# Attention scores of two heads issued together, their tiles in turn, in a two-block kernel on one core

## What is computed

```python
q, k, v, cb, cc, cx, ga, gb = jnp.split(rms_norm(x, g) @ w_in[l], splits, axis=-1)
q = partial_rope(q.reshape(b, s, 16, 64), cos, sin)     # 16 heads of 64
k = partial_rope(k.reshape(b, s, 4, 64), cos, sin)      # 4 key heads, one for 4 heads
sc = jnp.einsum('bqkgd,bskd->bkgqs', qi, ki) * scale    # the scores: 256 queries x 256 keys a head
sc = jnp.where(mask, sc, NEG_INF)
m = jnp.maximum(jnp.max(sc, axis=-1, keepdims=True), sink_f)
p = jnp.exp(sc - m)
o = einsum('bkgqs,bskd->bqkgd', p / (sum(p) + exp(sink_f - m)), vi)
```

## Time and profile before

| | |
|---|---|
| median of three timed runs | 2644.65 us (2629.52 to 2653.48) |
| profiled execution, first to last instruction (span) | 2638.4 us |
| TensorE matmul busy | 2328.1 us, 88% |
| VectorE busy | 1728.6 us, 66% |
| ScalarE busy | 972.9 us, 37% |
| chain that ended last, TensorE's share | 54% |
| one of the two loops of 16 steps | about 124 us (from 90.8 to 214.8 us) |

### The profile page before, as it was taken

The page is one execution under the profiler, slowest core; times in us unless marked ns, Lnnn a source line. Parts: engine busy times, 40 slices in busy tenths (PEclk is TensorE's granted clock), DMA queues, the critical chain, the costliest instruction groups (busy, mean ns, idle before and its releaser), DMA issues.

```text
span 2638.4 us, 33375 instructions
## 1 busy us (share of the span) xinstructions
PE 2328.1 (88%) x11926; PEld 1622.5 (61%) x11926; DVE 1728.6 (66%) x3439; ACT 972.9 (37%) x2088; POOL 682.4 (26%) x631
## 2 busy tenths in 40 slices
PE   8999999999999999898877799987798999777777
PEld 7999999899999979785322244463343446232222
DVE  5687677768677767666975555547954654954444
ACT  4444433453443345322322224413324732322222
POOL 0000001000000100023545433324423333455543
PEclk9999999999999999999999999999999999899999
DMA  7545477664547754169999999999999998999998
GB/s 298 199 160 196 163 277 282 249 246 155 193 148 279 284 196 160 68 236 382 403 419 422 421 411 391 401 390 407 413 401 373 395 395 325 383 412 421 422 421 354
DMA packets 110513, 828.14 MB, mean 314 GB/s; under 512 B 14384, under 2 KB 15296, under 8 KB 30992
## 3 DMA queue, kind: packets, MB, share of 16 engines
q0 software_dynamic: 90000, 595.97, 56.1%
q1 hardware_dynamic: 20352, 230.08, 23.2%
HBM read 824.95 MB, written 1.05 MB: 313 GB/s over the span
## 4 chain that ended last, share of the span: by engine, by line
PE 54%; DMA 18%; DVE 14%; ACT 5%; issue 4%; POOL 1%; DVEq 1%; ACTq 1%; PEldq 0%; SPq 0%; PEld 0%; POOLq 0%
PE pd L573 16%; PE pr L1124 12%; PE pa L573 11%; DMA ring_b<-in_peer_uv,eidx 9%; DMA wring<-in_peer_uv,eidx 6%; PE pr L573 6%; PE pa L1144 3%; DVE ring_b L2457 3%; PE pa L1238 2%; DVE wring L2457 2%; DVE wring_r L1774 1%; PE pd L1144 1%; DMA wring<-in_w_mix 1%; ACT junk L1539 1%; DMA aring<-in_ada_rows 1%
## 5 line engine op out<-in xcount | busy, mean ns | idle before, releaser
L1124 PE MATMUL pr<-ring_b,junk 128*128 128x512 f32 x976 | 464.2, 622 | 112.2 <-ACT junk L1539 111.6
L1124 PE MATMUL pr<-wring,junk 128*128 128x512 f32 x968 | 451.4, 611 | 105.2 <-ACT junk L1539 99.8
L1718 POOL DMA_INDIRECT ring_b<-in_peer_uv,eidx x244 | 294.4, 1207 | 597.1 <-PE pr L1124 348.3
L2457 DVE CUSTOM_DVE_ANT_0 wring<-wring,hrow 128x1024 f32<-128x1024 f32 x242 | 293.7, 1223 | 218.9 <-DMA wring<-in_peer_uv,eidx 210.9
L2457 DVE CUSTOM_DVE_ANT_0 ring_b<-ring_b,hrow 128x1024 f32<-128x1024 f32 x244 | 295.8, 1224 | 201.6 <-DMA ring_b<-in_peer_uv,eidx 195.3
L1124 PEld LDWEIGHTS pr<-ring_b,junk 128*128 128x128 f32 x976 | 184.3, 197 | 373.9 <-issue 197.2
L1124 PEld LDWEIGHTS pr<-wring,junk 128*128 128x128 f32 x968 | 178.3, 192 | 360.8 <-issue 188.1
L1718 POOL DMA_INDIRECT wring<-in_peer_uv,eidx x242 | 291.8, 1206 | 417.3 <-PE pr L1124 359.1
L1530 ACT ACTIVATE gel<-dots 128x2 f32<-128x2 f32 x255 | 51.6, 203 | 657.2 <-DVE dots L2457 655.4
L1702 POOL DMA_DIRECT2D aring<-in_ada_rows x112 | 60.2, 538 | 871.1 <-DVE adal L1867 870.9
L573 PE MATMUL pd<-hhi,wring_r 128*128 128x256 f32 x1024 | 222.1, 281 | 0.0
(11 more groups left out here) (393 smaller groups left out, 4358.7 us busy)
## 6 DMA issues: line engine op xcount, KB each, us to landing
wring<-in_w_mix SPq DMA_DIRECT2D x38, 2048.0 KB, 8.7
aring<-in_ada_rows POOLq DMA_DIRECT2D x112, 512.0 KB, 5.3
wring<-in_w_stick SPq DMA_DIRECT2D x24, 2048.0 KB, 9.4
wring<-in_w_ffn SPq DMA_DIRECT2D x22, 2048.0 KB, 8.7
wring<-in_w_lstm SPq DMA_DIRECT2D x12, 2048.0 KB, 8.3
wring<-in_w_back SPq DMA_DIRECT2D x8, 2048.0 KB, 8.5
wring<-in_w_back SPq DMA_DIRECT2D x4, 1536.0 KB, 6.8
ring_b<-in_peer_uv,eidx POOLq DMA_INDIRECT x244
```

Source lines behind the costliest of these rows:

```text
L1124: m = nc.tensor.matmul(pr[half][:, :], diag[:, q % DIAGS, :], row(q)[:, D + half * 512:D + (half + 1) * 512], start=(q % PICKS == 0), stop ...
L1718: pool.indirect_dma_start(out=row(q), out_offset=None, in_=ins["peer_uv"], in_offset=bass.IndirectOffsetOnAxis(ap=eidx[:, tt % NT, p:p + 1 ...
L2457: m = nc.vector.tensor_tensor_reduce(out=row(q)[:, 0:D], in0=row(q)[:, 0:D], in1=hrow[:, q // PICKS % NT, :], scale=1.0, scalar=0.0, op0=A ...
```

## The change

`scores` becomes `scores_of_two(h)`. It is called behind every second unit, in the even steps, and issues both the even head `h` and the odd head `h + 1`: tile 0 of the even head, tile 0 of the odd head, tile 1 of the even one, tile 1 of the odd one. The wait on `sc_read` counts one more head (both banks must be read), and that on `qk_ready` is for the second signal of the layer. Each head still signals `sc_full` on its last matmul. In odd steps no scores are issued. Nothing is changed on the other engines.

```diff
-                def scores(h):
+                def scores_of_two(h):
                     if h == 0:
-                        pe.wait_ge(qk_ready, l + 1)
-                    pe.wait_ge(sc_read, l * HEADS + h + 1)
-                    b0 = (h % 2) * HD
+                        pe.wait_ge(qk_ready, 2 * l + 2)
+                    pe.wait_ge(sc_read, l * HEADS + h + 2)
                     for t in range(NT):
-                        m = mm(psc[h % 2][:, t * SEQ:(t + 1) * SEQ], qT[b0:b0 + HD, h // 2, t * P:(t + 1) * P],
-                                             kT[b0:b0 + HD, h // GROUP, :], start=True, stop=True)
-                    m.then_inc(sc_full, 1)
+                        for a in range(2):
+                            b0 = a * HD
+                            m = mm(psc[a][:, t * SEQ:(t + 1) * SEQ], qT[b0:b0 + HD, h // 2, t * P:(t + 1) * P],
+                                   kT[b0:b0 + HD, h // GROUP, :], start=True, stop=True)
+                            if t == NT - 1:
+                                m.then_inc(sc_full, 1)
...
-                    scores(s)
+                    if s % 2 == 0:
+                        scores_of_two(s)
```

## The result

The changed kernel takes 2624.24 us (median of 20 runs, 2616.51 to 2641.60), the kernel before 2639.44 us (median of 20 runs, 2629.52 to 2657.13). The ratio is 0.9952 with a 95% interval of 0.9936 to 0.9968, so 12.7 us less, between 8 and 17 (the two medians by themselves differ by 15.2 us). The forecast was 13.3 us less, and 2631.4 us in a range of 2617 to 2653. Sign and size came out as forecast. The steps behind them did not all: the overlap follows another rule than the forecast's and saves more, the edges save more, and the waits that follow cost more. What was missed in the gains and in the loss cancels in part.

A forecast was written before the change was run, and what follows sets the result against it. The prediction took TensorE alone to bound the first layer's loop, repeated in the second. Saved edges 4.3 plus overlap 10.4 less waits 1.4 gave 13.3 us, from 2644.65 to 2631.4 us, range 2617 to 2653.

The forecast's parts named there:

- Step 1, the edges: Entering and leaving a head's scores on TensorE costs 0.27 us; sixteen groups vanish, saving 4.3 us.
- Step 2, the overlap: In a pair's scores, passes on different row halves join in order: eight take five places, saving 10.4 us.
- full overlap: Rival: the two heads' score passes interleave completely into four places; 15.4 us less, 2629.3 us; chance 5%.
- Step 3, the added wait: Before a pair's scores, waiting on `sc_read` for one head more, and on `qk_ready`, costs nothing.
- Step 4, what is late next: TensorE waits 0.7 us a layer at head 9's transposes for exponentials behind VectorE's steps; 1.4 us lost in all.
- no overlap: Rival: a pair's eight score passes run one behind the other; only edges save, 4.3 us, 2640.3 us; chance 25%.
- slower: Rival: each turn between row halves inside a pair costs 0.19 us; 4.8 us more, 2649.5 us; chance 12%.
- given back: Rival: VectorE's pace over the loop, or late slots, leave nothing of the gain; 2644.65 us; chance 8%.

The follow-up runs named there:

- e2_same_rows: The changed kernel, but the odd head's score matmuls read partitions 0 to 63 like the even head's; ratio to before 0.9970, loops 120.7 and 120.8 us.

## Why the prediction held, and where its steps did not

**What bounds the loop** was right: TensorE alone, and what it saves goes into the end of the loop. The gain is handed on to the second loop: the stretch between the loops takes 350.7 us before, 351.0 in the changed kernel and 349.8 in its second profile. Behind the loops no single span can show it (1949.1 us before, 1948.7 and 1953.4 in the two profiles of the changed kernel), but the timed ratios, 0.9952 and 0.9935 (12.7 and 17 us less), agree with all of the 15.9 us arriving.

**Step 1, the edges**, was right in kind and too small: 0.38 us a vanished group instead of 0.27, 16 x 0.11 = 1.8 us missed. The mis-sized term is the gap in front, which I took against the wrong neighbour.

**Step 2, the overlap**, failed in its rule. "Starts and ends stay in order, so pass 3 joins pass 2": the starts do not stay in order. Eight passes take four places, not five, and not because of the turns: with the heads in series it is the same. It was the rival *full overlap* that happened, to which I gave 5%, and its 15.4 us less is what the loops show (15.9). Its term is 16 x 0.86 = 13.8 us instead of 10.4. The row from which I drew the doubt, the two heads of the recurrent mixer, was set aside as a change of height that says nothing on two operands of 64 rows. That fits what was measured between 128 and 64 rows; no run was made on its 8 rows.

**Step 3, the added wait**, was right: no wait on `sc_read` or `qk_ready` appears.

**Step 4, what is late next**, was right in place and mechanism (exponentials of heads 7 to 9, behind VectorE's steps), and too small because the steps ahead of it were: 1.4 us forecast, 4.0 measured. With the true 1.24 us a pair, its own rows give the waits. Head 7 is reached 2.5 us early with 1.9 to spare, 0.6 too early; head 9 is 3.7 us early with 2.0 to spare, 1.7 in all. Measured is 1.8. The prediction doubled the first layer's rows, but in the second layer of the kernel before there is less to spare, 1.5 us at head 7 and 1.7 at head 9: 2.0 in all, and 2.2 measured.

The sum is then 6.1 (edges) + 13.8 (overlap) - 4.0 (waits) = 15.9 us, against 4.3 + 10.4 - 1.4 = 13.3. Two gains too small by 5.2 us and a loss too small by 2.6: that they cancel by half is luck, and so is it that the timed 12.7 us lies still nearer to the forecast than the loops' 15.9 do. The timed ratio, 8 to 17 us, holds both; it is the loops that tell them apart. The forecast's absolute time started from a median of three runs, 2644.65 us, which the median of 20 puts at 2639.44; the 2631.4 us were too high by 7.2 us, and 5.2 of them come from there.

The rivals *no overlap* and *slower* are excluded by the 1.06 us of a pair, and *given back* by the loops and by a ratio whose interval ends at 0.9968. The first is what e2_same_rows built. For the second, the starts show that a turn costs no more than 7 ns.

## What to carry to other kernels

Two small contractions that use different halves of the rows and different banks should be issued next to each other: here eight fp32 passes of 64x256 cost what four did, and the order among them was of no account. Group work of the same height, since each change from 128 rows to 64 and back cost 0.37 to 0.39 us here, with nothing waiting. And before such a gain is counted, walk the next engine's own rows forward by the gain: from step 4 to step 9 VectorE takes 43.3 us before and after the change (from one `lower` to the other, 125.57 to 168.85 and 122.09 to 165.37), TensorE took 41.2, which cost nothing yet, and needs 38.1 without waits. That took a fifth of the gain, and moving VectorE's work to its idle steps brought it back.

## What had not been expected of the hardware

- Matmuls on different halves of the rows start out of the program's order: with four passes of the even head ahead of four of the odd one, the starts still came in twos, 13 ns apart (7 ns where they were issued in turn).
- Two overlapped fp32 passes of 64x256 cost each other nothing: each has 376 ns (480 each head's first in a pair), as alone, and the pitch stays 0.216 us.
- A group of matmuls of 64 rows between work of 128 rows costs 0.37 to 0.39 us beside its passes. Whether the two heads could also write one bank was not tried.
